# Five small reorderings in a one-core hybrid decoder layer: key rotation, attention and retention steps, cache-score units, two Strassen adds, and one dropped table preload

## What is computed

```python
xn = rms_norm(x, norm1)
aq, ak, av, bq, bk, bv, bg, cx, cg, dq, dk, dv, dr, da = split(xn @ w_in)
A: differential attention (4 heads, 2 maps each; the samples over 2048 cached keys)
B: retention: rotary(bq), rotary(bk) * 64**-0.5, decay matrix, states, group norm, * silu(bg)
C: width-4 causal convolution of cx, RG-LRU, * gelu(cg)
D: gated linear attention (dq, dk, dv, da), rms norm, * silu(dr)
gates = sigmoid(xn @ w_merge + b_merge)              # one per branch and channel
h = x + sum_n(gates[n] * (branch[n] @ w_branch[n])) @ w_out
y = h + hierarchical_moe(rms_norm(h, norm2))         # top group, top 2 of its 4 experts
```

## Time and profile before

| what | value |
|---|---|
| device time, median of 3 runs | 796.54 us |
| the three runs | 793.12, 796.54, 798.35 us |
| the profiled execution, its own time | 793.12 us |
| span of the profiled execution | 791.2 us |
| PE busy | 764.1 us, 97% of the span |
| DVE, ACT, POOL busy | 383.7, 225.2, 295.6 us |
| mean granted PE clock | 0.989 of full |

### The profile page before, as it was taken

The page is one execution under the profiler, slowest core; times in us unless marked ns, Lnnn a source line. Parts: engine busy times, 40 slices in busy tenths (PEclk is TensorE's granted clock), DMA queues, the critical chain, the costliest instruction groups (busy, mean ns, idle before and its releaser), DMA issues.

```text
span 791.2 us, 14293 instructions
## 1 busy us (share of the span) xinstructions
PE 764.1 (97%) x5269; PEld 546.8 (69%) x5269; DVE 383.7 (48%) x714; ACT 225.2 (28%) x436; POOL 295.6 (37%) x221
## 2 busy tenths in 40 slices
PE   9999999999999999999999999999999799999992
PEld 7887678776677888777777787888887644333330
DVE  4637766777488689544544112734533722030210
ACT  4131443441423355132414222422201521020100
POOL 0000322254654984354424554534241122332314
PEclk9999999999999999999999999999999999999997
DMA  9352752345655542145544463351670899999943
GB/s 366 114 161 82 212 164 83 106 156 164 176 178 179 176 153 67 58 159 168 175 139 130 144 183 135 100 191 69 239 292 13 324 329 413 374 387 371 383 137 50
DMA packets 72538, 148.32 MB, mean 187 GB/s; under 512 B 13335, under 2 KB 47144, under 8 KB 70420
## 3 DMA queue, kind: packets, MB, share of 16 engines
q1 hardware_dynamic: 65716, 135.43, 49.3%
q0 software_dynamic: 5920, 10.82, 5.5%
q10 hardware_dynamic: 832, 1.16, 0.6%
HBM read 137.71 MB, written 18.90 MB: 198 GB/s over the span
## 4 chain that ended last, share of the span: by engine, by line
PE 88%; DVE 6%; ACT 2%; DMA 1%; issue 1%; POOLq 0%; SPq 0%; POOL 0%; DVEq 0%; ACTq 0%
PE ps L875 22%; PE ps L608 14%; PE ps L1211 10%; PE ps L844 7%; PE ps L1119 6%; PE ps L1281 5%; PE ps L651 3%; PE ps L623 3%; PE ps L901 2%; PE ps L597 2%; PE ps L1200 1%; PE ps L678 1%; PE ps L694 1%; PE ps L707 1%; PE ps L951 1%
## 5 line engine op out<-in xcount | busy, mean ns | idle before, releaser
L608 PE MATMUL ps<-xn,ring 128*128 128x268 f32 (+1 forms) x576 | 137.9, 395 | 0.2 <-ACT qk L1374 0.2
L608 PEld LDWEIGHTS ps<-xn,ring 128*128 128x128 f32 x576 | 108.1, 192 | 25.1 <-issue 4.2
L2574 POOL TENSOR_TENSOR kv<-kv,sgd 128x1024 f32<-128x1024 f32 (+1 forms) x32 | 81.0, 2548 | 101.8 <-DVE tmp L1848 58.0
L1532 ACT ACTIVATE sgt<-sgt,vec 128x260 f32<-128x260 f32 x60 | 30.1, 510 | 122.9 <-DVE sgt L2130 70.8
L2689 POOL DMA_INDIRECT out_y<-cst,gtab x24 | 37.3, 1555 | 70.8 <-DVE cst L2499 42.8
L844 PE MATMUL ps<-br,ring 128*128 128x260 f32 x256 | 60.9, 386 | 0.6 <-DVE sgt L2134 0.6
L875 PE MATMUL ps<-xn,ring 128*128 128x260 f32 x240 | 58.0, 385 | 0.0
L875 PE MATMUL ps<-xn,qb 128*128 128x260 f32 x240 | 57.6, 383 | 0.1
L844 PEld LDWEIGHTS ps<-br,ring 128*128 128x128 f32 x256 | 47.9, 190 | 11.2 <-issue 3.2
L1876 DVE TENSOR_REDUCE sgd<-kv 128x32 f32<-128x1024 f32 (+1 forms) x32 | 40.8, 1280 | 20.4 <-POOL kv L2574 20.4
L875 PEld LDWEIGHTS ps<-xn,qb 128*128 128x128 f32 x240 | 45.4, 190 | 7.4 <-issue 0.4
(11 more groups left out here) (526 smaller groups left out, 1500.9 us busy)
## 6 DMA issues: line engine op xcount, KB each, us to landing
ring<-in_w_mg SPq DMA_DIRECT2D x32, 640.0 KB, 4.8
kv<-in_kc SPq DMA_DIRECT2D x128, 128.0 KB, 2.1
kv<-in_vc SPq DMA_DIRECT2D x128, 128.0 KB, 2.1
ring<-in_w_in SPq DMA_DIRECT2D x24, 512.0 KB, 4.7
kv<-in_w SPq DMA_DIRECT2D x8, 1024.0 KB, 13.4
br<-in_w SPq DMA_DIRECT2D x7, 1024.0 KB
sgd<-in_w SPq DMA_DIRECT2D x6, 1024.0 KB
qk<-in_w SPq DMA_DIRECT2D x6, 1024.0 KB, 12.5
```

The source lines that it names most:

```text
L608: mm = pe.matmul(ps[:, 2 * (t % 2) + h, 0:hw], wsl(c, k), xnv[:, k, col0 + h * hw:col0 + (h + 1) * hw], start=(k == 0), stop=(k == KT - 1))
L1532: act.activation(g, g, ACT.Sigmoid, bias=vv(V_BM + 8 * "ABCD".index(n) + m + i)).then_inc(g_a, 1)
L2574: pool.tensor_tensor(kb, kb, qbc[:, b:b + 1, :].to_broadcast([P, HALF // 2 + (half and u), 256]), ALU.mult)\
```

## The change

Five places change; no arithmetic does.

1. Attention step 16 goes from the mid of `CG1` to the end of `CG0`, step 17 from the end of `CG1` to its mid; the two waits of retention step 1 go to step 0.
2. ACT's one-element square root after `V0` is taken out.
3. DVE does `rotate(0)` and `rotate(1)` ahead of `last_keys`.
4. The cache-score unit that DVE reduced after the retention keys is reduced ahead of them (`K_RET` ends in 3 instead of 2).
5. `adds(6, "V")` goes ahead of `sample_states`, `adds(7, "V")` ahead of the reciprocal of `dsd`.

```diff
-        "CX0": (11, 12), "CX1": (13, 14), "CG0": (15, -1), "CG1": (16, 17)}
+        "CX0": (11, 12), "CX1": (13, 14), "CG0": (15, 16), "CG1": (17, -1)}
...
-K_RET = [0, 0, 1, 2, 2, 1, 1, 0, 1, 2]
+K_RET = [0, 0, 1, 2, 2, 1, 1, 0, 1, 3]
...
                 if r == 0:
                     pe.wait_ge(rot_ok, 4)
                     pe.wait_ge(sexp, 32)
-                if r == 1:
                     pe.wait_ge(swt_ev, 16)
                     pe.wait_ge(sav_ev, 8)
...
-                    if i == 0:
-                        act.activation(sc[:, 54:55], eps, ACT.Sqrt)
...
+            rotate(0)
+            rotate(1)
             last_keys()
-            rotate(0)
             at_k = 0
             for s in range(18):
...
-                if s == 1:
-                    rotate(1)
...
             ins.then_inc(kd_ok[0], 1)
-            at_k = sampled(at_k, 1)
...
             keys()
+            adds(6, "V")
             sample_states()
-            adds(6, "V")
             adds(6, "22")
...
             adds(7, "U")
+            adds(7, "V")
             dve.wait_ge(pj_free, EV["DOS"] + 1)
             link(dve.reciprocal(dsd, dsd))
-            adds(7, "V")
             adds(7, "22")
```

## The result

The changed kernel takes 798.47 us (median of 22 runs, 796.63 to 803.26), the kernel before 793.46 us (median of 22, 791.29 to 798.35, the three shown at first among them). The ratio is 1.0063, with a 95% interval of 1.0049 to 1.0077: slower by 0.6%, 5.0 us. The forecast was 803.0 with a range of 798.5 to 808.0, so the measured median lies at the very edge of the range, 0.03 us outside it.

A forecast was written before the change was run, and what follows sets the result against it. PE, busy 97% of the span, was taken as the bound. Terms 0.8 + 1.8 + 1.3 + 1.2 + 1.4 = +6.5 us took the profiled 793.1 to 799.6, and from the 796.5 median to 803.0 us; range 798.5 to 808.0.

The forecast's parts named there:

- rival (a): Attention step 0: no slow stretch follows the new wait for scores 0; sum 4.7 us, time 801.2 us; chance 0.24.
- The prediction's own sign of being wrong: Whole kernel: wrong if PE's waits grow by less than 4 us, or its busy time by over 3 us.
- PE loses 0.8 us: Mean squares after `V0`: the square root table load comes late, so `AMS2` waits until 55.65 instead of 54.85.
- 2.8 - 2.8 + 1.8 = +1.8 us: Attention: new wait 2.8 at scores 0, step 3's wait and slow stretch gone -2.8, new clock fall +1.8.
- I take the slow stretch behind it to go as well: Behind attention step 3: the half-clock stretch, 1.8 us lost, ends together with the 0.99 us wait.
- I take it that the clock falls here instead: Attention step 0: the clock falls behind the new 2.8 us wait, +1.8 us.
- The 0.8 us for a held `combine(1)`: Early attention: POOL's product may hold `combine(1)`'s last instruction, up to 0.8 us; left out of the sum, kept in the range.
- PE waits 1.3 us: End of `CG0`: transposes 15 wait for the last instruction of `combine(15)`, 1.3 us, bounds 1.0 to 1.7.
- DVE's chain here already ends last: +1.2: Retention keys: PE already waits 1.10 us for DVE, so the 1.20 us unit adds +1.2 us.
- 0, if PE's delay of edit 1 lets DVE arrive with that much lead: Retention keys: lower bound for the moved unit's cost, 0 us; the upper bound was 1.5.
- Rival (b): More slow stretches behind waits at `kd_ok` and `CG0`, each up to 1.8 us; sum 8.3 or 10.1; chance 0.26.
- +1.4" (0.45 + 0.95): V adds: sample products of pair 7 wait 0.45 us, work behind pair 8's reciprocal is 0.95 late; bounds 1.0 to 1.8.

The follow-up runs named there:

- edit 3 alone: Kernel before with only rotations 0 and 1 put ahead of `last_keys`; ratio 1.0018, 796.60 us against 794.42.
- edit 1 alone: Kernel before with only attention steps 16 and 17 one place earlier and the two waits at retention step 0; ratio 0.9983, 794.29 us against 794.42.
- Edits 1 and 4 alone: Kernel before with only the earlier attention steps (ratio 0.9983), or only the cache-score unit ahead of the retention keys (1.0063); with both, 0.9985.
- alone, edit 4: Kernel before with only the cache-score unit reduced ahead of the retention keys; ratio 1.0063, 800.79 us against 794.42.
- edit 5 alone: Kernel before with only both V adds moved earlier; ratio 1.0027, 795.45 us against 794.22.

## Why the prediction was right or wrong

**Direction right, mechanism right for edits 1, 2 and 5 and in part for 3, wrong for 4.** Every wait was foreseen at its line and with its releaser, though two of them (pair 8 and the retention keys) at about two and three times their size. The forecast by the profiled execution's own time, 799.6, stands 2.4 above the 797.2 that the profile of the changed kernel took: +6.5 forecast, +4.1 there, +5.0 in the medians, +3.8 at equal clock. It is nearest to rival (a), +4.7, and its condition came true: no slow stretch behind the new wait. That its sum came so near is partly luck, as errors in both directions follow. Term by term, forecast to timeline: edit 2 0.8 to 0.94, edit 3 +1.8 to -0.32 in that pair of profiles (+1.2 without slow stretches), edit 1 1.3 to 1.72, edit 4 +1.2 to -0.41, edit 5 1.4 to 0.63. With +1.2 for edit 3 that is 4.1 instead of 6.5. The prediction's own sign of being wrong, waits that grow by less than 4 us, is met or not by what one counts: 5.3 over the page, 3.8 at the places of the change.

**The base: wrong by 3.1 us.** I added 3.4 to come from the profiled execution to "the median of the runs", 796.5. That median of three was 3.1 above the median of 22, 793.46. Of 91 later executions of the kernel before 17 took 798 us or more. Three runs out of such a mixture don't fix its median. This step alone is 3.1 of the 4.5 between 803.0 and 798.5; the other 1.5 is the sum, +6.5 against +5.0.

**Edit 2, "PE loses 0.8 us": right.** 0.88 at the wait, 0.94 in the timeline. The load took 1.28 us, began 0.02 behind ACT's last copy, and the square root began 0.01 behind it. The Trainium skill (ScalarE: Activation LUTs, section What ACT_TABLE_LOAD costs) gives about 2.66 us for a switch with its drain. This trace doesn't bear that out: no drain shows on either side of the load, and PE lost a third of that figure.

**Edit 3, "2.8 - 2.8 + 1.8 = +1.8 us": near, by two errors that cancel in part.** The wait was 2.43 (scores 0 came 2.57 late). The step "I take the slow stretch behind it to go as well" failed: one profile of eight has that stretch, so there is typically nothing to win. The step "I take it that the clock falls here instead" was a toss: it fell in the profile of edit 3 alone and not in that of the whole change, and where it fell it cost 3.1 us, not 1.8. Without either, the term is 2.43 - 0.99 and 0.2 of small change, +1.2. The Trainium skill (TensorE: Matmul & The Clock Gate, section on HAM oscillation) says that idle gaps throttle PE again; the runs agree with it only as something that can happen, since a gap of 2.4 us did and didn't, and the fall at 251 us with edit 1 alone had no gap ahead of it. The 0.8 us for a held `combine(1)` did not come. The reading of the clock left out a third stretch, at half clock over the last dozen microseconds of the kernel; every profile has one there, so nothing hangs on it.

**Edit 1, "PE waits 1.3 us": the wait right (1.32), the term too small.** PE's timeline moved by 1.72. The moved step splits one run of projection matmuls more. From start to start and without the wait, three runs of 16 take 11.3 us (3.77, 3.71, 3.81) where one of 32 and one of 16 took 10.9 (7.23, 3.71): the one cut more is most of the other 0.4.

**Edit 4, "DVE's chain here already ends last: +1.2": this step failed.** With edit 1 in place that chain does not end last. The keys' wait did not grow from 1.10 to 2.3; it shrank to 0.69. I had named the bound that happened ("0, if PE's delay of edit 1 lets DVE arrive with that much lead") and had not taken it. The way was another than that lead, though: DVE waits for PE in the retention rounds in both kernels, and what PE's delay changes is where DVE's recurrence lies against POOL. The operations of lines 1937 and 1918 took 2.18 and 2.77 us before, 1.26 and 1.56 in the changed kernel; that is 2.13 less, 0.46 of it idle, and 1.10 + 1.13 for the unit - 1.67 gives 0.56 where 0.69 was measured. Edits 1 and 4 alone show the coupling: the keys' waits are 0 and 2.07, together 0.46. And what I had not seen at all: alone, edit 4 costs 6.4 us by the medians, most of which I put down to the long slow stretch. Rival (b) had the place ("the waits at `kd_ok`") but priced a fall at up to 1.8; there it is 6.1.

**Edit 5, "+1.4" (0.45 + 0.95): the first right, 0.44; the second too large, 0.19.** The sum of what waits behind V was right, but the D norm of 1.38 that I carried along was a collision with POOL that the delay dissolved. I had bounded this edit below by 1.0; the true value lay under the bound.

**Sum of the timeline's terms, without slow stretches:** 0.9 + 1.2 + 1.3 (1.72 of edit 1 less 0.41 at the keys) + 0.6 = 4.0, against 3.8 measured at equal clock.

Open is why the clock falls in some executions and not in others after the same wait.

## What to carry to other kernels

An edit that delays PE by a microsecond shifts DVE against POOL: carry the undisturbed duration of an operation as one bound, and price each wait with the edits ahead of it in place. A wait that grows may be dear by what the clock does behind it, not by its own length, so look at which matmuls stand there. And take the base of a forecast of a few microseconds from many executions: what a single profile shows once, as a slow stretch, is no property of the kernel until a second profile has it.

## What the runs showed of the hardware that was not expected

- A slow stretch has no fixed price. Behind the keys' wait it lasted 13.6 us and cost 6.1 us, over the retention states (128x64 results), 64 products with one column and some projection matmuls; at 83 us of edit 3 alone it lasted 6.8 us and cost 3.1; at 97 us of the kernel before it lasted 3.4 us and cost 1.7, over projections. Each time it cost half its length or a little less.
- The clock can fall without a wait: at 251 us of edit 1 alone, with PE working without a break since 243.3, just behind a group of small products.
- After one and the same wait of about 2.4 us the granted clock was 0.50 in one profile and 1.00 in another, over the same matmuls.
- DVE operations with two SBUF inputs took 0.6 to 2 us longer beside POOL operations (0.75 to 1.38, 1.26 to 2.18, 0.72 to 2.75), and a shift of 1 us of the schedule decided which of them was hit. Each ended 0.1 to 0.2 us less than its undisturbed time after POOL's operation did (0.56 after 431.77, 1.13 after 223.58, 0.57 after 91.48), however much earlier it had begun. It can go the other way: in the profile of edit 5 alone POOL's product begins at 220.96 and DVE's operation at 220.97; DVE takes its 1.27, and POOL 3.49 instead of 2.36.
